# A chunked RWKV scan: the odd chunks' results in the other head's half of the partitions, and the small couplings in two parts

## Chip, core and metric

The kernel runs on one core of a Trainium2 chip. The metric is the device time of one execution in microseconds. TensorE is called PE here and VectorE DVE; ACT is ScalarE, POOL is GpSimd, and SP issues the loads.

## What is computed

The kernel runs a small model end to end: a transformer layer with pooling and neighbourhood attention, a layer with an RWKV mixer, and two conformer layers, over 512 latent and 256 context tokens of width 1024. The change touches the RWKV scan alone. For each of 16 heads (64 wide) and for both time directions the reference does this, first over the context, then over the latent tokens, which alone give an output:

```
def wkv_scan(s0, decay, k, v, kk, a, r, reverse):
    ...
    def step(S, inp):
        w_t, k_t, v_t, kk_t, kka_t = inp[:5]
        S = (S * w_t[:, :, None, :]
             - jnp.einsum('bhij,bhj->bhi', S, kk_t)[..., None] * kka_t[:, :, None, :]
             + v_t[..., None] * k_t[:, :, None, :])
        y = jnp.einsum('bhij,bhj->bhi', S, inp[5]) if emit else None
        return S, y
    S, ys = lax.scan(step, s0, xs, reverse=reverse)
```

## The kernel before

The 768 tokens are cut into 12 chunks of 64 (`C`). The heads are taken in 8 pairs; the two heads of a pair (`h`) lie in the two halves of the 128 partitions, `half(h)`. A pair has three groups (`g`) of four chunks: group 0 is the context, groups 1 and 2 are latent. `t` counts the 24 groups of all pairs. The chunks of a group are in two tiles `q` of two; `pos` is the parity of a chunk within its tile. The two directions `d` walk through the chunks in opposite order, so at each step of the scan they stand at chunks of opposite parity.

Two kinds of work are interleaved, in an order that `rwkv_steps` writes out by hand. For each of 12 places `k` it issues `prep(t, 0, k)`, then one part of `scan(t - 1, ...)`, then `prep(t, 1, k)`, then features of the next head pair and the readout of the last. Every engine goes through the same order, in its own queue, and waits on semaphores.

`prep` makes what a group needs without knowing the state. At k = 0 PE computes the small couplings (L1763: 8 matmuls of 64x64, each with its rows and its output in `half(h)`), which DVE copies through a mask into `xt` (L3569), and then the big ones (L1773: 8 matmuls from 64 rows into all 128 columns), which DVE multiplies by a mask into `couple` (L3579, in the context group L3581), one instruction for each head. At k = 1 PE transposes the small ones (L1814), which ACT copies (L2472), and multiplies the masked couplings with the values (L1787), which ACT copies to `bv` (L2449). From k = 2 to 9 a triangular inverse is doubled level by level: PE product (L1823), DVE masked copy (L3587), PE products (L1836, L1840), ACT copy (L2459). Its last level works on quarters of a block (L1827, L1851), with copies by ACT (L2466) and DVE (L3595). `home(level, h, pos)` says in which half of the partitions the inverse of a chunk lies after a level. For odd chunks it alternates from level to level; at `FULL_STEPS` = 4 it is `h`.

`scan` takes one step of four in three parts. Part 0: PE multiplies the state with the keys, the from-state product (L1864, 4 matmuls into bank 6), and DVE adds `bv` to make the residual `w_sb` (L3613). Part 1: PE multiplies it with the inverse (L1874), and ACT copies the result into `uv` (L2480). Part 2: PE computes the update of the state (L1886) and, in latent groups, the output `y` in bank 7 (L1893, L1898); DVE adds to the state (L3620, L3622) and takes y from its bank (L3628 or L3632), which signals `y_read`. The step's place k for part 0 is 0, 3, 6 or 9.

The features use L1907, L1914 and L1920 on PE, L3646, L3693 and others on DVE. A matmul of f32 shows in the trace as two weight loads and two matmul records, so 4 matmuls are x8.

## Time and profile before

| | us |
|---|---|
| median of 3 runs | 4571.34 (4560.85 to 4578.11) |
| the profiled execution | 4574.23 |
| its span, first to last instruction | 4572.4 |
| PE busy, weight loads busy | 4407.4, 3153.2 |
| DVE busy, ACT busy, POOL busy | 2697.3, 1026.2, 253.7 |
| mean granted clock of TensorE | 0.987 |

Busy times are sums over the span. The ends of matmuls are modelled, so the weight loads (PEld) show better when PE was issuing. The scan is one stage of the span, from 1340 to 1977 us.

### The profile page before, as it was taken

Reading aid. Unit: us, or ns where it says so; the run is one execution under the profiler, and the core shown is the slowest. Engines: PE = TensorE matmul, PEld = TensorE weight load, DVE = VectorE, ACT = ScalarE, POOL = GpSimd, SP = SyncE. Lnnn points to the kernel's source line nnn. Section 1 sums busy time; section 2 is a strip of 40 time slices with the busy share of each in tenths; the row PEclk is TensorE's granted clock in tenths of the full one; section 3 lists DMA queues with packets and bytes.
Section 4 is the critical chain, followed back from the end, with each engine's and each line's share of the span. In section 5 each row is a group of like instructions: output and inputs, shape, how many; then the busy total and the mean of one; then the engine's idle time right before and its main releaser. Section 6 shows DMA issues by size and latency. Waiting matters only on the chain.

```text
span 4572.4 us, 76195 instructions
## 1 busy us (share of the span) xinstructions
PE 4407.4 (96%) x32648; PEld 3153.2 (69%) x32648; DVE 2697.3 (59%) x4804; ACT 1026.2 (22%) x2222; POOL 253.7 (6%) x355
## 2 busy tenths in 40 slices
PE   8999999999999999999999999989999999989998
PEld 4555655555547777768886888557886888556887
DVE  3173555536348888745565666655667666664656
ACT  1063000002037666630002100341001100251000
POOL 0001000001001111110000000210000000120000
PEclk9999999999999999999999999999999999999999
DMA  5320222211200000122221222212222222212221
GB/s 213 132 81 37 92 111 111 110 56 56 88 1 4 4 4 4 40 84 74 93 92 70 82 92 83 74 56 74 93 88 88 77 90 83 92 38 85 81 92 46
DMA packets 27071, 339.47 MB, mean 74 GB/s; under 512 B 3024, under 2 KB 3024, under 8 KB 6896
## 3 DMA queue, kind: packets, MB, share of 16 engines
q1 hardware_dynamic: 24048, 324.51, 18.8%
q0 software_dynamic: 2688, 10.09, 0.6%
q8 instruction: 259, 4.24, 0.4%
q14 instruction: 76, 0.62, 0.0%
HBM read 330.40 MB, written 4.19 MB: 73 GB/s over the span
## 4 chain that ended last, share of the span: by engine, by line
PE 87%; DVE 7%; ACT 3%; issue 2%; DMA 0%; SPq 0%; DVEq 0%; ACTq 0%
PE ps L1624 48%; PE ps L1233 21%; PE ps L1242 2%; PE ps L1286 1%; PE ps L1773 1%; PE ps L1387 1%; ACT arena L2216 1%; PE ps L1480 1%; PE ps L1557 1%; PE ps L1703 1%; PE ps L1907 1%; PE ps L1836 1%; PE ps L1448 1%; PE ps L1513 1%; PE ps L1460 1%
## 5 line engine op out<-in xcount | busy, mean ns | idle before, releaser
L1624 PE MATMUL ps<-arena 128*128 128x256 f32 (+1 forms) x9096 | 2102.4, 393 | 1.8 <-DVE arena L3243 1.8
L1624 PEld LDWEIGHTS ps<-arena 128*128 128x128 f32 x9096 | 1725.8, 190 | 365.4 <-issue 12.4
L1233 PE MATMUL ps<-arena 128*128 128x512 f32 (+3 forms) x2816 | 997.9, 515 | 0.4 <-DVE arena L2819 0.4
L1233 PEld LDWEIGHTS ps<-arena 128*128 128x128 f32 x2816 | 524.3, 190 | 460.0 <-issue 396.6
L3234 DVE TENSOR_TENSOR arena<-ps,arena 128x512 f32<-128x512 f32 (+1 forms) x250 | 157.5, 630 | 302.7 <-PE ps L1624 300.8
L3234 DVE TENSOR_TENSOR square<-ps,square 128x512 f32<-128x512 f32 (+1 forms) x145 | 99.1, 683 | 174.4 <-PE ps L1624 174.4
L3175 DVE TENSOR_TENSOR arena<-arena 128x1024 f32<-128x1024 f32 (+2 forms) x153 | 190.5, 1245 | 3.3
L2383 ACT COPY square<-ps 128x512 f32<-128x512 f32 (+1 forms) x65 | 37.2, 572 | 648.6 <-PE ps L1624 581.4
L2383 ACT COPY arena<-ps 128x384 f32<-128x384 f32 (+1 forms) x35 | 18.6, 530 | 577.5 <-PE ps L1624 546.5
L2459 ACT COPY arena<-ps 128x512 f32<-128x512 f32 x192 | 110.7, 586 | 68.2 <-PE ps L1840 64.8
L3243 DVE TENSOR_TENSOR arena<-arena 128x1024 f32<-128x1024 f32 (+1 forms) x60 | 72.5, 1208 | 86.9 <-ACT square L2383 76.7
L1624 PE MATMUL ps<-arena,square 128*128 128x256 f32 (+1 forms) x432 | 122.0, 431 | 0.0
L2216 ACT ACTIVATE arena<-arena,state_sum 128x256 f32<-128x256 f32 (+3 forms) x128 | 76.5, 601 | 195.3 <-DVE state_sum L2800 195.2
L1242 PE MATMUL ps<-arena 128*128 128x256 f32 (+1 forms) x336 | 105.2, 475 | 15.1 <-DVE arena L3018 8.4
L1167 POOL COPY square<-const 128x256 f32<-128x256 f32 x144 | 80.4, 560 | 700.9 <-PE ps L1840 472.0
L3234 DVE TENSOR_TENSOR reset<-ps,square 128x512 f32<-128x512 f32 (+1 forms) x65 | 43.9, 675 | 127.5 <-PE ps L1624 127.5
L2374 ACT ACTIVATE reset<-arena 128x256 f32<-128x256 f32 x40 | 16.7, 417 | 420.2 <-DVE arena L3308 420.2
L3230 DVE TENSOR_TENSOR arena<-arena 128x1024 f32<-128x1024 f32 (+2 forms) x100 | 107.6, 1076 | 3.4
L3249 DVE TENSOR_TENSOR arena<-arena 128x1024 f32<-128x1024 f32 (+2 forms) x100 | 107.0, 1070 | 1.1
L1624 PEld LDWEIGHTS ps<-arena,square 128*128 128x128 f32 x432 | 82.1, 190 | 33.3
L2746 DVE SCALAR_TENSOR_TENSOR arena<-arena,vec 128x512 f32<-128x512 f32 x120 | 103.5, 901 | 1.3
L1086 POOL TENSOR_TENSOR arena<-arena 128x512 f32<-128x512 f32 x60 | 72.0, 1200 | 566.4 <-ACT arena L2183 559.8
(395 smaller groups left out, 5123.2 us busy)
## 6 DMA issues: line engine op xcount, KB each, us to landing
arena<-in_panels SPq DMA_DIRECT2D x144, 2048.0 KB, 7.7
arena<-in_panels SPq DMA_DIRECT2D x9, 1536.0 KB, 6.4
arena<-in_bias POOLq DMA_DIRECT2D x8, 512.0 KB, 4.3
arena<-in_x_in SPq DMA_DIRECT2D x1, 3072.0 KB, 10.7
x_save<-arena POOLq DMA_DIRECT2D x1, 2048.0 KB, 7.5
arena<-x_save POOLq DMA_DIRECT2D x1, 2048.0 KB, 14.0
out_x<-arena SPq DMA_DIRECT2D x8, 256.0 KB, 2.9
arena<-in_panels SPq DMA_DIRECT2D x1, 1792.0 KB, 11.6
```

The costliest lines, as they stand in the source:

```text
L1167: pool.tensor_copy(step_sb[d][level % 2], unit).then_inc(sem("step_unit"), one("step_unit"))
L1233: ins = pe.matmul(dest, left(k), right(k), start=(k == 0), stop=(k == nk - 1))
L1242: ins = pe.matmul(bank[:, 0:b - a], w[:, k, m * P:(m + 1) * P], src[:, k, a:b], start=(k == 0), stop=(k == KD - 1))
L1624: ins = pe.matmul(bank[:, j * cut.side:(j + 1) * cut.side], left[:, k, j * P:(j + 1) * P], right[k], start=(k == 0), stop=(k == cut.rows - 1))
L2216: act.activation(p_h, p_h, ACT.Exp, bias=soft_at(i, h, NEGMAX), scale=-1.0, accum_out=soft_at(i, h, SUM)).then_inc(sem(f"exped{h}"), one(f ...
L2459: act.copy(both_sb[par][d], both_banks(d)[:, :, P:3 * P].rearrange("p a (w x) -> p a w x", w=2)).then_inc(sem(f"x_ready{d}"), one(f"x_read ...
L2746: ins = dve.scalar_tensor_tensor(conv_y[:, c, :], src, w, conv_y[:, c, :], ALU.mult, ALU.add)
L3175: ins = dve.tensor_tensor(part, x[:, rows], y[:, rows], op)
L3230: dve.tensor_tensor(a21, left_block(w, 0, 0, c), a21, ALU.subtract).then_inc(sem("left"), one("left"))
L3234: dve.tensor_tensor(out, product_of(tile(), cut), other, ALU.add).then_inc(sem("tile_free"), one("tile_free"))
L3243: dve.tensor_tensor(a11, left_block(total, 0, 0, cut), a11, ALU.subtract).then_inc(sem("tile_free"), one("tile_free"))
L3249: dve.tensor_tensor(a12, a12, a11, ALU.subtract).then_inc(sem("left"), one("left"))
```

## The change

The results of odd chunks (`pos` = 1) move to the other half of the partitions: `home` is shifted by one level, so that it is `h ^ 1` at `FULL_STEPS` (`crossed`). The values, the last level of the inverse, the residual and the solve follow. The from-state product of direction d goes to bank 6 + d, so its four matmuls have four different pairs of input and output half; DVE reads the residual from two banks. Bank 7 is the one that holds y, and PE now waits for `y_read` before it writes there. The small couplings of even chunks stay ahead of the big ones; those of odd chunks, whose output lies in the other half, come behind them, after a wait for the first part. `small{d}` counts twice in each group, and DVE's masked copy waits for both.

```diff
@@ -712 @@
+        def crossed(h, pos):
+            return home(FULL_STEPS, h, pos)
@@ -732 @@
         def home(level, h, pos):
-            return h if pos == 0 else h ^ level % 2
+            return h if pos == 0 else h ^ (level + 1) % 2
...
         def plain_at(level, h, pos):
-            return h if level == 0 else home(level - 1, h, pos)
+            return home(max(level - 1, 0), h, pos)
@@ -1757 @@
                     bank = misc("small", t, d)
-                    for q, e, pos, c in places(d, g):
-                        o = (2 * q + pos) * C
-                        for h in range(2):
-                            ins = pe.matmul(ps[half(h), bank, o:o + C], bk[d][half(h), c // 2, 2 * e + pos, :],
-                                            kk_part(p % 2, d, c, h), start=True, stop=True)
-                    ins.then_inc(sem(f"small{d}"), one(f"small{d}"))
+                    def small(of):
+                        for q, e, pos, c in places(d, g):
+                            o = (2 * q + pos) * C
+                            for h in range(2):
+                                if pos == of:
+                                    ins = pe.matmul(ps[half(home(0, h, pos)), bank, o:o + C], bk[d][half(h), c // 2, 2 * e + pos, :],
+                                                    kk_part(p % 2, d, c, h), start=True, stop=True)
+                        ins.then_inc(sem(f"small{d}"), one(f"small{d}"))
+
+                    small(0)
 
                     if t > 0:
                         pe.wait_ge(sem(f"z_ready{d}"), 2 * t)
...
                     ins.then_inc(sem(f"big{d}"), one(f"big{d}"))
+
+                    pe.wait_ge(sem(f"small{d}"), 2 * t + 1)
+                    small(1)
@@ -1784 @@
-                            ins = pe.matmul(ps[half(h), 2 * d + pos, q * C:(q + 1) * C], couple[d][rows, 0, h, 2 * q + pos, :],
+                            ins = pe.matmul(ps[half(crossed(h, pos)), 2 * d + pos, q * C:(q + 1) * C], couple[d][rows, 0, h, 2 * q + pos, :],
                                             uv[par][d][rows, q, e, half(h)], start=True, stop=True)
@@ -1824 @@
-                        ins = pe.matmul(ps[shifted(C * h, second), 2 * d + pos, q * C // 2:(q + 1) * C // 2],
+                        ins = pe.matmul(ps[shifted(C * crossed(h, pos), second), 2 * d + pos, q * C // 2:(q + 1) * C // 2],
                                         left[rows, second], right[rows, first], start=True, stop=True)
@@ -1847 @@
-                    rows = shifted(C * h, second)
-                    ins = pe.matmul(ps[shifted(C * h, first), 2 * d, 2 * P + i * C // 2:2 * P + (i + 1) * C // 2],
+                    rows = shifted(C * crossed(h, pos), second)
+                    ins = pe.matmul(ps[shifted(C * crossed(h, pos), first), 2 * d, 2 * P + i * C // 2:2 * P + (i + 1) * C // 2],
                                     lx_sb[d][rows, pos, q, :], xt[t % 2][d][rows, at, q, second], start=True, stop=True)
@@ -1858 @@
                 if part == 0:
                     pe.wait_ge(sem("state"), step + 1)
+                    if n["y"] > 0:
+                        pe.wait_ge(sem("y_read"), n["y"])
                     for d in range(2):
                         q, e, pos, c = place(d, g, s)
                         for h in range(2):
-                            ins = pe.matmul(ps[half(h), 6, d * C:(d + 1) * C], kk_part(p % 2, d, c, h), state[half(h), buf, d, :],
-                                            start=True, stop=True)
+                            ins = pe.matmul(ps[half(crossed(h, pos)), 6 + d, 3 * P:3 * P + C], kk_part(p % 2, d, c, h),
+                                            state[half(h), buf, d, :], start=True, stop=True)
...
-                                            w_sb[half(h), d, :], start=True, stop=True)
+                                            w_sb[half(crossed(h, pos)), d, :], start=True, stop=True)
@@ -3565 @@
-                    dve.wait_ge(sem(f"small{d}"), t + 1)
+                    dve.wait_ge(sem(f"small{d}"), 2 * (t + 1))
@@ -3610 @@
-                    dve.tensor_tensor(w_sb[:, :, :], chunked(ps[:, 6, 0:P]), each, ALU.add).then_inc(
+                    dve.tensor_tensor(w_sb[:, :, :], ps[:, 6:8, 3 * P:3 * P + C], each, ALU.add).then_inc(
                         sem("residual"), one("residual"))
```

## Rows read from the trace of the kernel before

**Rows 1.** Windows: core, stretch, its us, busy of PE, PEld, DVE, ACT, POOL (records), clock.
```profile
1340.00:1977.00 637.00, 583.70 (x16838) 446.38 (x16838) 490.54 (x1130) 412.62 (x933) 106.91 (x191) 0.97 0.03 10
```

**Rows 2.** Waits in the scan stage: who waited for whom, us, times, longest.
```profile
PEld ps L1787 <- DVE arena L3579: 6.2, 16, 0.4
```

**Rows 3.** Timeline of one latent group's start: start us, us, engine, line, what, [idle before].
```profile
1597.09 0.55 PEld L1763 LDWEIGHTS ps<-arena 64*64 64x64 f32 x16
...
1597.70 0.97 PEld L1773 LDWEIGHTS ps<-arena 64*128 64x128 f32 x16
...
1597.92 0.45 DVE L3569 COPY_PREDICATED arena<-const,ps 128x256 f32<-128x256 int32 x1
...
1598.79 0.31 PEld L1864 LDWEIGHTS ps<-state,arena 64*64 64x64 f32 x8
1598.79 0.45 PE L1864 MATMUL ps<-state,arena 64*64 64x64 f32 x8
1598.91 1.29 DVE L3579 TENSOR_TENSOR arena<-ps,const 128x512 f32<-128x512 f32 x2 [0.53 <-PE ps L1773]
1599.02 0.55 PEld L1763 LDWEIGHTS ps<-arena 64*64 64x64 f32 x16
...
1600.11 0.28 DVE L3613 TENSOR_TENSOR w<-ps,arena 128x128 f32<-128x128 f32 x1
...
1600.72 0.20 PEld L1814 LDWEIGHTS ps<-const,arena 128*128 128x128 f32 x2
...
1600.85 1.29 DVE L3579 TENSOR_TENSOR arena<-ps,const 128x512 f32<-128x512 f32 x2
1601.09 0.32 PEld L1787 LDWEIGHTS ps<-arena 64*64 64x64 f32 x16 [0.17 <-issue]
...
1601.32 0.21 PEld L1874 LDWEIGHTS ps<-w,arena 64*64 64x64 f32 x8
...
1602.19 0.33 PEld L1787 LDWEIGHTS ps<-arena 64*64 64x64 f32 x16 [0.38 <-DVE arena L3579]
```

**Rows 4.** Chain that ended last, 1545.5 to 1624: start us, us, what.
```profile
1592.01 0.17 PE ps L1864 x6
...
1606.67 0.15 PE ps L1864 x5
```

**Rows 5.** Lines of the scan stage: shapes, count, busy us, mean ns, idle before and releasers.
```profile
L3587 DVE COPY_PREDICATED square<-const,ps 128x256 f32<-128x256 int32 x144 | 63.6, 442 | 40.9 <-PE ps L1823 37.9 <-POOL square L1167 1.5
...
L1864 PEld LDWEIGHTS ps<-state,arena 64*64 64x64 f32 x768 | 31.1, 135 | 7.2 <-issue 2.5 <-DVE state L3606 1.7 <-DVE state L3622 0.3
...
L3569 DVE COPY_PREDICATED arena<-const,ps 128x256 f32<-128x256 int32 x48 | 21.2, 442 | 1.8 <-PE ps L1763 1.1
...
L1874 PEld LDWEIGHTS ps<-w,arena 64*64 64x64 f32 x768 | 20.4, 133 | 17.0 <-DVE w L3613 15.1 <-issue 0.8
```

**Rows 6.** Timeline of a context group's start (the columns of rows 3).
```profile
1571.81 0.54 PEld L1763 LDWEIGHTS ps<-arena 64*64 64x64 f32 x16
...
1575.46 0.76 DVE L3581 TENSOR_TENSOR arena<-ps,const 128x256 f32<-128x256 f32 x2 [0.52 <-PE ps L1773]
...
1576.59 0.32 PEld L1787 LDWEIGHTS ps<-arena 64*64 64x64 f32 x16 [0.17 <-issue]
...
1577.07 0.37 ACT L2472 COPY arena<-ps 128x256 f32<-128x256 f32 x1
```

**Rows 7.** Timeline around a from-state product that follows a copy of y.
```profile
1563.91 0.28 DVE L3628 COPY arena<-ps 128x128 f32<-128x128 f32 x1
1564.05 0.31 PEld L1864 LDWEIGHTS ps<-state,arena 64*64 64x64 f32 x8
...
1566.86 0.21 PEld L1874 LDWEIGHTS ps<-w,arena 64*64 64x64 f32 x8 [1.43 <-DVE w L3613]
```

**Rows 8.** The same chain as in rows 4, at a group's start in which DVE comes late.
```profile
1547.24 0.36 DVE arena L3569
...
1550.67 0.46 PE ps L1787 x16
```

## Prediction, made before the changed kernel was run

> **What bounds the kernel now.** I read the views in this order: the windows, to find how much of the span the change can touch; the waits inside that stage; the timeline of one chunk group; the chain that ended last. All matmuls that change lie in the scan stage, 1340 to 1977 us, 637 of 4572.4 us [rows 1]. There PE is busy 583.70 us by the modelled ends, but its weight loads only 446.38, and DVE is busy 490.54. So PE is not simply full: it runs in short bursts and hands over to DVE and ACT between them. The waits say to whom: its loads stood still for 6.2 us, in 16 places, for DVE's coupling mask L3579 [rows 2]; the rows by line add 15.1 us for the residual L3613, and for the state only 1.7 us [rows 5]. The stage is 24 chunk groups (8 head pairs, 3 groups each), each some 25 us long, and in each the three engines take turns. A nanosecond taken from PE counts only where the chain of work that ended last runs through PE at that place.
>
> **What one burst costs.** I count each matmul as two records, since an f32 product is loaded twice: 4 matmuls are x8. The from-state product (L1864, x8) uses two of the four 64x64 quarters of the array and takes 0.23 us from its first load to the next line's (1598.79 to 1599.02). The coupling values (L1787, x16, all four quarters) take the same 0.23 us for twice the records (1601.09 to 1601.32) [rows 3]. So four quarters halve the time: x8 costs 0.11 instead of 0.23. The small couplings (L1763, x16, two quarters) take 0.61 us to the first load of the big ones. Eight of the 16 are 0.23, so the other eight and the change of tile shape are 0.38, of which some 0.15 is the change of shape.
>
> **Part 1, the product from the state: the gain.** The two directions always stand at chunks of opposite parity, so with the odd chunk crossed over, the four matmuls of a step fall into four quarters and two banks. There are 96 steps. The most this can give is 96 x (0.23 - 0.11) = 10.6 us, rounding 0.11 kept. But it counts only on the chain. In a whole head pair (1546 to 1624, 12 steps) the chain names L1864 at four steps, of which two rows stand here [rows 4]. At two of the four it is the step inside the k = 0 burst (as at 1598.79 [rows 3]), which part 2 covers. At 1592.01 and 1606.67 PE work follows it, and the saving reaches ACT's copy. At the other eight the chain is on DVE or ACT: the masked copy of the first direction, a reciprocal, an activation. So I keep 2 x 8 x 0.11 = 1.8 us.
>
> The residual L3613 now reads two banks instead of one. The trace has no such residual, but the masked copy L3587 reads two banks and L3569 one, both 128x256, at 442 ns each [rows 5]. I take zero for it; had it a price, it would be DVE time in 96 places, and 10 ns each would be 1 us.
>
> The inverse, the values, the last half product and the solve only exchange halves: the number of matmuls, their shapes and the quarters in use stay the same, and both layouts already occur today, at levels 0 and 1. Zero, with nothing that must hide it.
>
> **Part 2, the small couplings in two parts: the cost.** Today DVE's copy L3569 starts when the small couplings are there, and runs beside the big ones: it lies at +0.83 us from the start of the burst (1597.92 after 1597.09), the mask L3579 can start only at +1.82 when the big ones are done, and DVE stands idle 0.53 us between [rows 3]. So this copy is free now. After the change the second half of the small couplings comes behind the big ones, and the copy waits for it. I lay out one group, with zero at its first small load. PE: first half 0 to 0.38, big to 1.47 (1.09, as 1597.70 to 1598.79), second half to 1.70, from-state product to 1.81. Then direction 1: first half to 2.19, big to 3.28, second half and change of shape to 3.66, where today it is 3.63. So PE itself is even. DVE: eight such records are finished 0.45 us after their first load and DVE starts 0.05 later, so the first copy starts at 1.47 + 0.50 = 1.97. The mask follows 0.36 later (the share of L3569 in a chain that is all DVE [rows 8]), at 2.33, the residual 1.20 later, 3.53, and then the second copy at 3.28 + 0.50 = 3.78 (DVE would be ready at 3.73). The second mask runs 4.14 to 5.44 (1.30), and the values matmul of direction 1 (L1787) starts at 5.48. Today it starts at 1602.19, which is 5.10. Behind this wait stand, on PE's queue, all of the next level's matmuls, and on DVE the features: all move by 0.38. The wait of PE for this mask exists in 16 places [rows 2], the two latent groups of each of 8 pairs: 16 x 0.38 = 6.1 us.
>
> In the context group the masks are half as long (0.76 for two). There the values of direction 1 start at +4.78 (1576.59 after 1571.81), and PE isn't waiting for DVE. By the same layout the mask ends at 4.90, and those values move by 0.17, to 4.95. But ACT, which must copy their result, is busy with L2480 and L2472 until 1577.44, and the chain goes through ACT [rows 6]. Zero there, but 0.03 of PE: 8 x 0.03 = 0.2 us.
>
> The new wait of PE between big and second half is for its own first half, finished 0.45 us after its start while the big ones load for 0.97: satisfied long before, so nothing. Its price without that cover would be the 0.45 us.
>
> **Part 3, the wait for y_read.** The from-state product now also writes the bank from which DVE takes y. DVE's copy of y follows the state in its queue. At most steps DVE is done with y before PE comes. At one step in each pair PE starts while y is still being copied (L3628 from 1563.91 for 0.28, L1864 at 1564.05): there it starts 0.19 us later, with 0.05 for the hand-over. Queued behind it on PE are the two level-3 products of direction 1 and the halves L1827. But PE then idles 1.43 us for the residual, which DVE reaches only after its features [rows 7]. Zero; uncovered it would be 8 x 0.2 = 1.6 us.
>
> **Sum.** +6.1 + 0.2 - 1.8 = +4.5 us. The profiled execution took 4574.23 us (span 4572.4 and 1.83 around it), so 4578.7 on its own terms. That execution lay 2.9 us above the median 4571.34 of the three shown, which gives 4575.8, so 4576 us.
>
> The Trainium skill, "TensorEngine Tiling (Array Packing)", section Key Properties, says that changing the tiling mode drains the engine. The trace agrees: 0.15 us at small to big. The change adds one such switch in each of 24 groups, from the second half to the transposes. The page alone would count them all, 24 x 0.15 = 3.6 us; in the layout above they lie inside DVE's lag.
>
> **The rivals.**
> A: the whole gain is kept and the copy is hidden. For it: DVE idles 0.53 and 0.52 us before masks [rows 3, 6]. Against it: that idle lies in front of the very point to which the copy moves, so it is used up by the copy's new wait. It gives 4571.3 - 10.6 = 4561 us.
> B, the slower side: DVE's lag at k = 0 is not 0.38 once but both copies in full, in all 24 groups, and the change of shape too. That would be 24 x (2 x 0.44 + 0.15) = 24.7 us, 4596 us. It decides if the big products are ready before DVE comes to them at both directions, context groups included. For it: in every third group DVE comes late to the burst (L3728, then L3569 at 1547.24) and the chain is all DVE from there to the values [rows 8]. Against it: DVE waits 0.52 us for PE in the context group [rows 6].
> C: the four quarters don't run side by side, or what they give is nowhere on the chain, and only the cost stays: 4571.3 + 6.3 = 4577.6, say 4578 us. For it: L1874, x8 over four quarters, has 20.4 us of loads against 31.1 of L1864 [rows 5], so they should; the chain is the weak link. The Trainium skill, same page, section PSUM Bottleneck, says that tiling speeds up TensorE but not the emptying of PSUM. By it the saving would vanish everywhere, with this same result; the trace agrees at eight of twelve steps.
>
> **How the numbers follow.** Forecast 0.60, its own range 4566 to 4586 (the two kept steps could be six or none, the lag 0.2 to 0.5 us in 16 to 24 groups, and the three runs before lie between 4560.85 and 4578.11). A 0.15, B 0.10, C 0.15, where C lies within the forecast's range. The range to 8 in 10 is 4561 to 4590: it takes in A's end and leaves B out. A measurement of this kernel can tell 0.5%, 22.9 us, from no change: below 4548.5 would be faster, above 4594.2 slower. A does not reach the first; B's end lies just beyond the second. So faster 0.03, same 0.90, slower 0.07.
>
> **What would show it.** After the change: L1864's loads, x8, some 0.20 us in a burst instead of 0.31; L3569 at about +1.97 from the first L1763, without idle DVE time between it and the first mask; the wait of L1787 for L3579 grown from 0.38 to about 0.75 at 16 places; the stage about 4 us longer than 637. Wrong if the wait at L1787 doesn't grow (the copy is hidden: A), if it grows in the context groups too (B), if L1864 stays at 0.31 (C), or if a new wait shows in front of the second half of L1763 or of L1864 with y as its releaser.

## The result, and the profile after

| | before | after |
|---|---|---|
| median of 20 runs, us | 4570.56 (4560.85 to 4578.74) | 4579.84 (4569.53 to 4592.37) |
| profiled execution, its span | 4574.23, 4572.4 | 4576.36, 4574.5 |
| mean granted clock of that execution | 0.987 | 0.988 |
| PE, weight loads, DVE busy in the span | 4407.4, 3153.2, 2697.3 | 4396.6, 3140.8, 2694.2 |

The ratio after to before is 1.0022, with a 95% interval of 1.0016 to 1.0028: +9.3 us by the medians, where +4.5 was forecast. That is below the 0.5% named in the prediction, but clearly not zero. The change makes the kernel a little slower, although PE's loads are shorter by 12 us in the whole span (3153.2 to 3140.8).

The windows of the scan stage show where those went. This row is that of [rows 1], for the kernel after (core, stretch, its us, busy of PE, PEld, DVE, ACT, POOL with records, clock):

```profile
1340.00:1977.00 637.00, 571.55 (x16793) 434.15 (x16794) 486.07 (x1126) 414.18 (x933) 104.84 (x191) 0.97 0.03 10
```

Weight loads fall from 446.38 to 434.15 us, in a stage that is not shorter. The rows by line name the places. The line numbers have moved: L1769 is the small couplings (before L1763), L1877 the from-state product (L1864), L1887 the solve (L1874), L1798 the values (L1787), L3582 the masked copy (L3569), L3592 the coupling mask (L3579), L3626 the residual (L3613). Columns: shapes, count, busy us and mean ns, idle before and releasers, as in [rows 5].

```profile
L3626 DVE TENSOR_TENSOR w<-ps,arena 128x128 f32<-128x128 f32 x96 | 27.3, 284 | 7.2 <-PE ps L1877 6.1
L1877 PEld LDWEIGHTS ps<-state,arena 64*64 64x64 f32 x768 | 22.2, 135 | 6.9 <-issue 3.5 <-DVE state L3619 2.1 <-DVE state L3635 0.6
L3582 DVE COPY_PREDICATED arena<-const,ps 128x256 f32<-128x256 int32 x48 | 21.5, 447 | 34.4 <-PE ps L1769 34.4
L1887 PEld LDWEIGHTS ps<-w,arena 64*64 64x64 f32 x768 | 20.8, 135 | 17.5 <-DVE w L3626 15.7 <-issue 0.8
```

The loads of the from-state product fall from 31.1 to 22.2 us, to about those of the solve, which always used four quarters. Ahead of the masked copy DVE stood idle 1.8 us in all 48 places together [rows 5], now 34.4 us. In front of the mask it stood idle 11.3 us before and not at all now, so part of this is the same idle time at another place. The waits of the stage (us in total, times, longest) show what came of it on PE, to be held against [rows 2]:

```profile
PEld ps L1798 <- DVE arena L3592: 12.1, 16, 0.8
...
PEld ps L1798 <- DVE arena L3594: 1.8, 7, 0.3
```

The wait has kept its 16 places and grown from 6.2 to 12.1 us, by 5.9. The timeline of one latent group's start shows the mechanism (start us, us, engine, line, what, idle before):

```profile
1600.62 0.31 PEld L1769 LDWEIGHTS ps<-arena 64*64 64x64 f32 x8
...
1601.00 0.97 PEld L1781 LDWEIGHTS ps<-arena 64*128 64x128 f32 x16
...
1602.09 0.31 PEld L1769 LDWEIGHTS ps<-arena 64*64 64x64 f32 x8
...
1602.66 0.45 DVE L3582 COPY_PREDICATED arena<-const,ps 128x256 f32<-128x256 int32 x1 [1.23 <-PE ps L1769]
1602.76 0.97 PEld L1781 LDWEIGHTS ps<-arena 64*128 64x128 f32 x16
...
1603.00 1.28 DVE L3592 TENSOR_TENSOR arena<-ps,const 128x512 f32<-128x512 f32 x2
1603.85 0.31 PEld L1769 LDWEIGHTS ps<-arena 64*64 64x64 f32 x8
...
1604.42 0.45 DVE L3582 COPY_PREDICATED arena<-const,ps 128x256 f32<-128x256 int32 x1
...
1604.76 1.28 DVE L3592 TENSOR_TENSOR arena<-ps,const 128x512 f32<-128x512 f32 x2
...
1606.09 0.32 PEld L1798 LDWEIGHTS ps<-arena 64*64 64x64 f32 x16 [0.78 <-DVE arena L3592]
```

With zero at 1600.62: first copy at 2.04 (forecast 1.97), first mask 2.38 (2.33), second copy 3.80 (3.78), values of direction 1 at 5.47 (5.48, and 5.10 before). The copy that used to run beside the big couplings now starts when they are over, and the mask comes behind it.

**The account by groups.** These are the first loads of the three groups of one pair and of the next pair, first for before, then for after:

```profile
1495.63 0.55 PEld L1763 LDWEIGHTS ps<-arena 64*64 64x64 f32 x16
...
1520.85 0.54 PEld L1763 LDWEIGHTS ps<-arena 64*64 64x64 f32 x16
...
1545.57 0.55 PEld L1763 LDWEIGHTS ps<-arena 64*64 64x64 f32 x16 [0.76 <-issue]
```

The next pair starts at 1571.81 [rows 6]. After:

```profile
1498.28 0.31 PEld L1769 LDWEIGHTS ps<-arena 64*64 64x64 f32 x8
...
1523.59 0.31 PEld L1769 LDWEIGHTS ps<-arena 64*64 64x64 f32 x8
...
1548.57 0.31 PEld L1769 LDWEIGHTS ps<-arena 64*64 64x64 f32 x8 [0.76 <-issue]
...
1575.42 0.31 PEld L1769 LDWEIGHTS ps<-arena 64*64 64x64 f32 x8
```

Context group 25.22 before, 25.31 after (25.20 in other pairs); first latent group 24.72 and 24.98; second latent group 26.24 and 26.85. So the pair grew from 76.18 to 77.14, by 0.96 us, times 8 is 7.7 us. Other pairs scatter about this: the second latent group has 26.04 to 26.25 us before and 26.68 to 27.12 after. The first latent group grew by 0.26: the lag of 0.38, less the 0.11 of one from-state product on the chain, as forecast. The second grew by 0.61, and that was not forecast. A step of DVE there shows why. It is the sum over the keys, a product of two tiles in SBUF, L3682 before and L3695 after; by line and form, first before, then after:

```profile
L3682 DVE TENSOR_TENSOR arena<-arena 128x512 f32<-128x512 f32 x7 | 4.8, 681 | 0.0
```

```profile
L3695 DVE TENSOR_TENSOR arena<-arena 128x512 f32<-128x512 f32 x7 | 6.3, 903 | 0.0
```

The same work takes 903 ns instead of 681. The timeline shows what runs beside it; the last row of each fence has the shortest, median and longest time of POOL's two copies in ns. Before:

```profile
1554.49 1.65 POOL L1167 COPY square<-const 128x256 f32<-128x256 f32 x2 [12.21 <-PE ps L1840]
...
1555.20 0.68 DVE L3682 TENSOR_TENSOR arena<-arena 128x512 f32<-128x512 f32 x1
...
L1167 POOL COPY square<-const x2: 721/833/945, 1554.5 to 1555.2; 128x256 f32<-128x256 f32 x2
```

After:

```profile
1557.87 1.08 POOL L1170 COPY square<-const 128x256 f32<-128x256 f32 x2 [12.58 <-PE ps L1851]
...
1558.58 0.90 DVE L3695 TENSOR_TENSOR arena<-arena 128x512 f32<-128x512 f32 x1
...
L1170 POOL COPY square<-const x2: 397/566/734, 1557.9 to 1558.5; 128x256 f32<-128x256 f32 x2
```

POOL fills the tile for the next level with the unit matrix as soon as PE's last product of a level is done, for direction 0 first, then for direction 1. Before, the second copy ends at 1556.14 and takes 0.945 us, so it starts at 1555.195, 0.005 to 0.01 us ahead of the sum, and it is the copy that is stretched. After, it ends at 1558.95 and takes 0.397, so it starts at 1558.55, 0.03 ahead of the sum, and it is the sum that is stretched. The two lie beside each other in both kernels; what changed is by how much the copy comes first. PE's last product stands behind the from-state product on PE's queue, so with the shorter one it comes earlier (the records of L1851 end 0.23 us ahead of the sum, those of L1840 before 0.11), while DVE's queue has not moved. Of these 0.12 us the second copy moves by only 0.03; POOL's first copy runs until 0.02 us behind the sum's start in both kernels, which may be what holds it (not shown). In all seven pairs of after the copy is 0.03 us ahead and the sum takes 0.90 us; in before it is 0.01 ahead in six pairs and 0.24 behind in one, and the sum takes 0.68 in all. The run e1, which has the split but not the shorter product, shows the same as before, so it is the crossing that moves the copy. The run e11 tests what the order does.

### The profile page after: what moved, and what is told of

Same layout as the page of the kernel before. It is cut to its first block, busy times and chain, and to the rows that moved or that the text cites. A ratio compares the mean times of both kernels' runs of the same rounds, so it can differ in the third digit from the quotient of the medians.

```text
span 4574.5 us, 76286 instructions
## 1 busy us (share of the span) xinstructions
PE 4396.6 (96%) x32648; PEld 3140.8 (69%) x32648; DVE 2694.2 (59%) x4804; ACT 1027.8 (22%) x2222; POOL 252.1 (6%) x355
## 4 chain that ended last, share of the span: by engine, by line
PE 87%; DVE 7%; ACT 4%; issue 2%; DMA 0%; SPq 0%; DVEq 0%; ACTq 0%
PE ps L1627 48%; PE ps L1236 21%; PE ps L1245 2%; PE ps L1289 1%; PE ps L1390 1%; PE ps L1781 1%; DVE arena L3592 1%; PE ps L1560 1%; PE ps L1483 1%; ACT arena L2229 1%; ACT arena L2472 1%; PE ps L1706 1%; PE ps L1920 1%; PE ps L1451 1%; PE ps L1847 1%
```

## The experiments

Ratios are to the kernel before, run beside each; its medians were 4571.24 (with e0 to e3), 4570.36 (e4 to e7), 4569.95 (e8 to e10) and 4571.31 (e11). The fourth column is the time from the first load of the first of the 24 groups to that of the last, in the profiled execution (before 595.8, after 600.0). The last column is explained below the table.

| run | median us | ratio, 95% | 23 groups, us | over before at equal clock, us (estimate) |
|---|---|---|---|---|
| e0 the change, again | 4582.15 | 1.0020 (1.0010 to 1.0030) | 608.2 | +10.8 (2.0) |
| e1 split alone | 4583.49 | 1.0020 (1.0010 to 1.0030) | 607.3 | +10.8 (1.4) |
| e2 wait for y alone | 4569.78 | 0.9995 (0.9984 to 1.0005) | 593.7 | +1.8 (1.3) |
| e3 all small ones first | 4591.92 | 1.0036 (1.0023 to 1.0049) | 612.1 | +15.3 (2.5) |
| e4 the change, no POOL copies | 4573.48 | 1.0006 (0.9997 to 1.0014) | 593.5 | +3.0 (2.0) |
| e5 before, no POOL copies | 4557.15 | 0.9974 (0.9964 to 0.9984) | 582.3 | -7.0 (1.5) |
| e6 the change, masks first | 4571.98 | 1.0005 (0.9994 to 1.0015) | 594.9 | -1.3 (2.2) |
| e7 the change, key sum moved | 4586.51 | 1.0037 (1.0024 to 1.0049) | 610.8 | +11.5 (1.3) |
| e8 before, masks first | 4576.50 | 1.0018 (1.0009 to 1.0027) | 599.9 | +6.1 (1.4) |
| e9 split alone, masks first | 4571.81 | 1.0012 (1.0002 to 1.0022) | 606.7 | +1.8 (1.9) |
| e10 as e6, again | 4573.49 | 1.0006 (0.9997 to 1.0015) | 598.1 | -0.1 (1.7) |
| e11 the change, a copy later | 4579.21 | 1.0024 (1.0014 to 1.0033) | 607.9 | +7.0 (2.2) |

The fourth column wanders by several us for the same kernel (after 600.0 and 608.2, e6 and e10 594.9 and 598.1). The granted clock is at the lower of its two levels, 1.2 GHz, for short stretches, and a group with such a stretch is longer: in before, a first latent group with 1.7 us of it takes 25.54 instead of 24.72 us, a second latent group with 5.1 us of it 28.22 instead of 26.24. Each execution has them in other places; in the scan stage they add up to 44 us before, 41 after, 58 in e0, 55 in e6 and in e10. So lengths of groups are compared below only where no such stretch falls into them. These are the medians of such groups, in us, without the groups at the two ends of the scan, which differ from the others (a dash where there is none):

| kernel | context | first latent | second latent |
|---|---|---|---|
| before | 25.22 | 24.72 | 26.24 |
| after | 25.20 | 24.98 | 26.85 |
| e1 split alone | 25.37 | 25.27 | 26.80 |
| e2 wait for y alone | 25.22 | 24.72 | 26.26 |
| e5 before, no POOL copies | 25.32 | 24.71 | 25.55 |
| e6 the change, masks first | 25.19 | 24.37 | 26.10 |
| e8 before, masks first | 25.22 | 24.89 | 26.70 |
| e9 split alone, masks first | 25.37 | 24.66 | - |

The clock moves the medians too. In the 102 executions of before that were run beside these, those with a lower mean granted clock took longer, 2.8 us for each 0.001. The last column of the first table is an estimate from this: the mean of a run's executions over that of before beside it, both brought to the same mean clock, with two standard errors in brackets. It takes the clock as given and can't say whether a kernel itself had a part in it.

**e0_changed_again.** The change once more, beside the experiments.

> The changed kernel itself on the same chip, as a yardstick for the others. +7 to +12 us against before by the comparison of 20 runs; by the traces of one execution of each, +4 to +6 us in the scan stage.

4582.15 us against 4571.24: the loss stands, +10.9 by the medians and +10.8 at equal clock.

**e1_split_only.** The split of the small couplings with its two waits, and nothing crossed.

```diff
+                    def small(of):
+                        for q, e, pos, c in places(d, g):
...
+                                if pos == of:
+                                    ins = pe.matmul(ps[half(h), bank, o:o + C], ...
+                    small(0)
...
+                    pe.wait_ge(sem(f"small{d}"), 2 * t + 1)
+                    small(1)
...
-                    dve.wait_ge(sem(f"small{d}"), t + 1)
+                    dve.wait_ge(sem(f"small{d}"), 2 * (t + 1))
```

> The kernel before, with only the small couplings cut in two: even chunks ahead of the big ones, a wait, odd chunks behind them; nothing is crossed over and the from-state product stays in two quarters. Theory 1 (the masked copy loses its cover at k = 0): the second direction's values matmul waits 0.38 us longer for the mask in 16 groups, no gain comes from the from-state product, and no mask or feature of DVE is otherwise moved against POOL: +6 us against before. Rival (the loss comes from the waits for y or from the exchange of halves): +0 to +1 us. Rival B of the prediction (both copies uncovered in all groups): +20 us or more.

4583.49 us, +12.3 (+10.8 at equal clock, as e0): the split alone is as slow as the change. Its waits are those of the change (L1795 is the values there, L3587 the mask):

```profile
PEld ps L1795 <- DVE arena L3587: 12.1, 16, 0.8
```

The start of a latent group shows why more (zero at 1606.40):

```profile
1606.40 0.31 PEld L1766 LDWEIGHTS ps<-arena 64*64 64x64 f32 x8
...
1612.05 0.32 PEld L1795 LDWEIGHTS ps<-arena 64*64 64x64 f32 x16 [0.78 <-DVE arena L3587]
```

The values of direction 1 come at 5.65, not at 5.47: the from-state product between the two bursts still takes 0.23 us, so the second burst, and the copy behind it, come 0.11 later, and the rest goes to small shifts that I didn't separate. The lag is 0.55 us, and the first latent group grows by just that, 25.27 against 24.72. The pair from 1503.38 to 1580.83 lasts 77.45, 1.27 more than before, or 10 us for 8 pairs. So the expectation had the place right and the size too small: of the saving on the from-state product, the part inside the burst does count once the split is there. Held against e1, the change is shorter by 0.17 us in the context group and 0.29 in the first latent one; in the second the stretched sum takes the gain back.

**e2_y_wait_only.** Before, with the wait for the reading of y alone.

```diff
                     pe.wait_ge(sem("state"), step + 1)
+                    if n["y"] > 0:
+                        pe.wait_ge(sem("y_read"), n["y"])
```

> The kernel before, with only the wait for y_read ahead of the from-state product. Theory 1: nothing, within 1 us, since in the one step of each pair where PE comes before y is read it later idles 1.4 us for the residual. Rival: the wait passes through to the end, 8 x 0.2 = 1.6 us or, if PE stands at every latent step, up to 64 x 0.2 = 13 us.

Ratio 0.9995, and groups as long as before (25.22, 24.72 and 26.26). By the groups the wait costs nothing, as forecast. The estimate at equal clock, +1.8 (1.3), would allow the 1.6 us of the rival, but no group shows it.

**e3_both_parts_first.** The change, but both parts of both directions stand ahead of the big couplings, and DVE does both masked copies ahead of the masks. Within a group this should give back what the split costs.

```diff
+                    if d == 0:
...
+                        banks = [misc("small", t, to) for to in range(2)]
+                        for of in range(2):
+                            for to in range(2):
+                                if of:
+                                    pe.wait_ge(sem(f"small{to}"), 2 * t + 1)
+                                small(to, of)
...
+                    for to in range(2) if d == 0 else ():
+                        bank, _ = MISC[("small", t, to)]
...
+                        dve.copy_predicated(flat2(xt[par][to]), unit_mask(to), ...
```

> The changed kernel, with both parts of the small couplings of both directions ahead of the big ones (order: even chunks of direction 0, of direction 1, odd of 0, odd of 1, then big 0, from-state, big 1), and DVE's two masked copies ahead of the masks. Theory 1: the copies lie beside the big products again, the values wait for the mask no longer than before, and the gain of the from-state product stays; 16 x 0.38 and more is won back: 6 to 9 us less than the changed kernel, and 0 to 2 us less than before. Rival (the loss is elsewhere: y, crossing, POOL): as slow as the changed kernel, +9 us against before.

+20.7 us, about 10 worse than the change, where 6 to 9 less were expected: a miss. The waits of PE for the first small load name the cause (times, longest; L3745 is the gate of the last pair's readout, L2518 an activation of ACT):

```profile
PE ps L1765 <- DVE arena L3745: 10.4, 7, 1.7
...
PE ps L1765 <- ACT arena L2518: 3.2, 7, 0.7
```

```profile
1556.24 0.69 DVE L3745 TENSOR_TENSOR arena<-arena,ps 128x512 f32<-128x512 f32 x1
1557.05 1.08 PEld L1765 LDWEIGHTS ps<-arena 64*64 64x64 f32 x32 [2.53 <-issue]
```

The small couplings of direction 1 go to the second of two banks that are given out in turn (`misc`), and its last user is read only by those two steps. When its couplings come behind direction 0's big ones, the bank is free in time; at the head of the burst PE waits. This is a bank's cost and says nothing against the split as such: but the order in which all small ones come first isn't free either.

**e4_changed_no_pool and e5_before_no_pool.** POOL's copies of the unit matrix are left out of the change and of before. The levels of the inverse then work on tiles that are not reset; all other instructions are there.

```diff
-                level, part = divmod(k - 2, 2)
-                if part == 1 and 0 <= level < FULL_STEPS and ...
-                    pool.wait_ge(sem(f"z{d}"), LEVEL_STEPS * t + level + 1)
-                    step_unit(d, level)
...
-                    dve.wait_ge(sem("step_unit"), 2 * (FULL_STEPS * t + level) + d + 1)
+                    dve.wait_ge(sem("step_unit"), min(4, 2 * (FULL_STEPS * t + level) + d + 1))
```

> The changed kernel without the copies with which POOL refills the step tiles during the scan (left out: those copies, so the inverse is computed on stale tiles; times of all other instructions stand). Theory: in the changed kernel one POOL copy falls on DVE's k_sum product in each pair, which takes 0.90 us there instead of 0.68 before; without POOL it is 0.68 again, and this kernel is slower than the same cut of the kernel before by 6 us, not 8 (0.22 x 8 = 1.8 less). Rival: k_sum is longer for another reason and stays at 0.90; the distance stays at 8 us or more.

> The kernel before without the same POOL copies (left out: those copies; times of all other instructions stand). It is the yardstick for the run before it. The copies of before fall on other DVE instructions, so this is 0 to 6 us faster than before; k_sum takes 0.68 us as before.

The key sum in e4 (its L3691):

```profile
L3691 DVE TENSOR_TENSOR arena<-arena 128x512 f32<-128x512 f32 x7 | 4.8, 681 | 0.0
```

It is back at 681 ns, so it is POOL's copy that lengthens it, by 0.22 us. Seven of the 8 pairs have it in the scan (the sum for the first pair lies ahead of it), which is 1.5 us of the loss. The medians can't carry that figure: e4 and e5 lie 16 us apart, more than the change costs with the copies, not less, and e5 is 13 us faster than before where 0 to 6 were expected. Part of it is the clock (0.9876 and 0.9893 in the mean of their runs); at equal clock the distance is 10.0 us, that of e0 and before 10.8, and the errors of both are larger than 1.5. Undisturbed groups are 24.98 and 26.06 to 26.39 us (first and second latent) in e4 and 24.71 and 25.55 in e5, with the context even, so 0.8 to 1.1 a pair, 6 to 9 us. So the stretched sum is shown by its own time in e4, and its share of the kernel's time is an estimate.

**e6_masks_first.** If the cost is that the masked copy stands ahead of the mask on DVE's queue, it should vanish when they change places. Nobody waits at once for the copy but the transpose; so in direction 1 PE also does the values ahead of the transpose, and ACT copies `bv` ahead of it.

```diff
                 if k == 0:
-                    bank, _ = MISC[("small", t, d)]
-                    dve.wait_ge(sem("unit_set"), 2 * t + d + 1)
-                    dve.wait_ge(sem(f"small{d}"), 2 * (t + 1))
-                    dve.copy_predicated(z, unit_mask(d), ...
...
+                    bank, _ = MISC[("small", t, d)]
+                    dve.wait_ge(sem("unit_set"), 2 * t + d + 1)
+                    dve.wait_ge(sem(f"small{d}"), 2 * (t + 1))
+                    dve.copy_predicated(z, unit_mask(d), ...
...
                 elif k == 1:
+                    if d == 0:
+                        turn()
...
+                    if d == 1:
+                        turn()
```

> The changed kernel, with DVE's two masks ahead of its masked copy in both directions, and with the values matmul of direction 1 (and ACT's copy of it) ahead of the transposes. Theory 1: the masks no longer wait behind the copy, so the values of direction 1 start near +4.8 us after the burst's first load instead of +5.48; what then waits is the transposes, to about +5.15, so that the next level starts some 0.2 us earlier in 16 groups: 3 us less than the changed kernel. Rival (DVE's order has no share in the loss): no difference from the changed kernel.

4571.98 us, ratio 1.0005: 8 to 10 us less than the change, where 3 were expected. The timeline (zero at 1602.40; L3595 mask, L3603 masked copy, L1802 values, L1831 transpose):

```profile
1602.40 0.31 PEld L1769 LDWEIGHTS ps<-arena 64*64 64x64 f32 x8
...
1603.99 1.29 DVE L3595 TENSOR_TENSOR arena<-ps,const 128x512 f32<-128x512 f32 x2 [0.79 <-PE ps L1781]
...
1605.19 0.43 DVE L3603 COPY_PREDICATED arena<-const,ps 128x256 f32<-128x256 int32 x1
...
1605.75 1.29 DVE L3595 TENSOR_TENSOR arena<-ps,const 128x512 f32<-128x512 f32 x2
...
1606.96 0.44 DVE L3603 COPY_PREDICATED arena<-const,ps 128x256 f32<-128x256 int32 x1
1607.09 0.32 PEld L1802 LDWEIGHTS ps<-arena 64*64 64x64 f32 x16 [0.27 <-DVE arena L3595]
...
1607.48 0.20 PEld L1831 LDWEIGHTS ps<-const,arena 128*128 128x128 f32 x2
```

The first mask starts at 1.59 instead of 2.38, the values of direction 1 at 4.69 instead of 5.47. The first latent group takes 24.37 us (after 24.98, before 24.72), and the key sum is back at 682 ns: DVE's queue moved too, and the copy now starts 0.07 us behind the sum. This is the strongest evidence for the place of the loss.

**e7_changed_k_sum_moved.** The change, with the key sum and the bonus moved from k = 3 and 6 to k = 7, out of reach of that copy.

```diff
-... 3: [("exp", 1, 0), ("k_sum", 0, 0)],
+... 3: [("exp", 1, 0)],
...
-... 6: [("kr", 1, 2), ("bk", 0, 0), ("bonus", 0, 0)],
+... 6: [("kr", 1, 2), ("bk", 0, 0)], 7: [("k_sum", 0, 0), ("bonus", 0, 0)],
```

> The changed kernel, with the k_sum product and the bonus product after it moved from k = 3 and 6 to k = 7 of the third group of a pair. Theory: POOL's copy no longer meets k_sum, which takes 0.68 us again, and the masked copy behind it starts 0.2 to 0.5 us earlier in 8 groups: 2 to 4 us less than the changed kernel, if k = 7 has room. Rival: the stretch lost to POOL is off the chain, no difference; or k = 7 has no room, up to 8 x 1.4 = 11 us more.

4586.51 us, +16: a miss. The sum takes 878 ns at its new place too, where another copy of POOL has started ahead of it, and the second latent group is 27.20 us long (26.85). That fits the rival, that k = 7 has no room for it on DVE; it was not shown separately.

**e8_before_masks_first, e9_split_masks_first and e10_masks_first_again.** Is e6 faster because of its order alone, and does it need the split and the crossing? e8 is before with the order of e6, e9 is e1 with it, e10 is e6 again.

> The kernel before (one part of small couplings, nothing crossed) with the order of the run e6: DVE's masks ahead of its masked copy, the values of direction 1 ahead of its transposes. Theory: here the copy was free beside the big products, so moving it behind the masks only makes the transposes of direction 1 wait, to about +5.45 us after the burst's first load instead of +4.5: 2 to 6 us more than before. Rival (the order of e6 is better by itself, whatever the split): 5 to 8 us less than before.

> The kernel before with the small couplings in two parts and the order of e6, still with the from-state product in two quarters. Against e6 it lacks only the crossing, so the distance is what the four quarters give. Theory: 0.16 us in the k = 0 burst of 16 groups (the second direction starts 0.12 later, its odd part is late by the same) and 0.11 at one further step in two groups of each pair: 3 to 5 us slower than e6. Rival (the four quarters are nowhere on the chain): equal to e6.

> The run e6 again, beside the two others on the same chip. By the undisturbed groups in the trace of e6 it needs 75.6 us for a head pair where before needs 76.1 and the changed kernel 77.0: 4 us less than before and 11 less than changed; by the medians of e6, 1 to 2 us more than before. Whichever holds, it lies 7 to 11 us under the changed kernel.

In before the new order costs 6.5 us (pair 76.82 instead of 76.18): there the masked copy runs free beside the big couplings, and putting it behind the mask uncovers it. With the split it is the better order: 4571.81 for e9 against 4583.49 for e1. What the crossing then adds, e10 and e6 against e9, lies within the scatter of the medians (+1.7 and +0.2; ratios 1.0006 and 1.0005 against 1.0012). The undisturbed groups do show it: 25.19 against 25.37 in the context and 24.37 against 24.66 in the first latent group, 0.47 us a pair or 3.8 us, of the size that was expected. So the right order of DVE depends on where PE puts the small couplings. By the medians e6 and e10 are level with before, and no version beat it. Their groups would say 0.5 us a pair less than before, 4 us; at equal clock it is 1.3 (2.2) and 0.1 (1.7) us less. Whether the change with masks first is faster than before stays open.

**e11_copy_after_sum.** The change with all of POOL's copies, but the one that meets the sum waits for the residual of DVE, and so comes behind the start of the sum.

```diff
                     pool.wait_ge(sem(f"z{d}"), LEVEL_STEPS * t + level + 1)
+                    if t % GROUPS == 2 and k == 3 and d == 1:
+                        pool.wait_ge(sem("residual"), 4 * (t - 1) + 2)
                     step_unit(d, level)
```

> The changed kernel with one more wait: in the second latent group of each pair, at k = 3, POOL's copy of the unit matrix for direction 1 also waits for DVE's residual of that step. In the changed kernel this copy starts 0.03 us ahead of DVE's sum over the keys, and the sum takes 0.90 us; in the kernel before it starts 0.01 ahead, the sum takes 0.68 and the copy 0.94. The residual ends 0.08 us after the sum's start in DVE's queue, so the copy will now start behind the sum. All of POOL's copies stay. Theory 1, whichever of the two comes first is served first and the other one waits: the sum is back at 0.68 us in all pairs, the copy grows from 0.40 to 0.85 or more, the second latent group is 0.2 us shorter (26.65 instead of 26.85), and the kernel 1.8 us faster than the changed one by the groups, which the medians (4579.8 and 4582.2 before this) may not show. Theory 2, the two slow each other down for as long as they overlap, whoever comes first: the sum stays at 0.85 to 0.90 us, since the copy still lies beside it, and nothing is gained. Theory 3, the sum is lengthened by something else that moved with PE: it stays at 0.90 and the copy at 0.40.

```profile
1565.22 0.68 DVE L3697 TENSOR_TENSOR arena<-arena 128x512 f32<-128x512 f32 x1
1565.43 0.73 POOL L1170 COPY square<-const 128x256 f32<-128x256 f32 x1 [0.19 <-DVE w L3628]
```

The sum is back at 0.68 us, in all seven pairs, although the copy lies beside it for 0.47 us. The copy takes 0.73 instead of 0.40 and ends 0.26 us behind the sum. So theory 1 holds, with the case of before added: a lead of 0.01 us by the records was not enough for the copy, one of 0.035 us was. (The copy grew less than expected, since it starts 0.21 behind the sum; its end is where it was before.) The second latent group takes 26.62 us instead of 26.85 (1555.22 to 1581.84). The median, 4579.21, is level with that of the change, which 1.5 us can't alter visibly; at equal clock it is 3.8 us less than e0, with an error of 3.

## Why the prediction was right, and where its sum was short

**What bounds the stage.** Right. A nanosecond off PE counted only where the chain runs through PE: 8.9 us less of from-state loads, and the stage no shorter.

**Part 2, the lag.** Right in place and size: where the copy's uncovering was laid out, the runs show 16 waits for the mask, +5.9 us where +6.1 stood, each step of the laid-out group within 0.07 us, PE even. e1 shows that the split carries the loss, and e6, e8 and e9 that it is the order on DVE through which it does. Right too that the context group hides it: the seven waits for L3594 there come to 1.8 us, but the group is 25.20 to 25.31 us long, before 25.22. Without the crossing it isn't hidden in full: the context groups of e1 take 25.37.

**Part 1, the gain.** The mechanism is right: in the burst at k = 0 the x8 loads take 0.11 us to the next line's first load, before 0.23. Its sum of 1.8 us was too large. Of the two steps of a pair that I kept, the one in the first latent group counts in full (0.38 - 0.11 = 0.27, measured 0.26). The one in the context group, 1592.01 [rows 4], is not seen in the group's length: six undisturbed groups changed by -0.11 to +0.14, by 0.00 in the mean, where 0.03 - 0.11 = -0.08 was forecast. That is 0.08 us a pair, 0.6 us in all. The chain named the product, but its saving doesn't show at the group's end; into which later wait it went I did not isolate.

**The missed term.** The prediction asked of a shorter PE step only whether the chain moves. It also moved PE against DVE within the group, and with it POOL's copy, from 0.01 us ahead of a DVE instruction, where the copy pays, to 0.03 ahead, where the sum pays: 681 to 903 ns, 0.22 x 7 = 1.5 us. In e4, e6 and e11 the sum is back at 681 to 682 ns. The step that failed is the place of Part 1 where a saving off the chain was worth nothing; POOL's queue waits for the last product of a level, and nothing in the sum followed it.

**Together:** 4.5 + 1.5 + 0.6 is 6.6 us, against 7.7 by the groups of the pair shown and 6.7 by the medians of the undisturbed groups (76.18 and 77.03 a pair). The medians of the kernel say 9.3, with 7.3 to 12.8 by the interval of the ratio. Some of the rest lies in the first pair, whose first latent group is 22.81 us long in before and in e5 and 23.80 in e4, 1.0 more where the others have 0.26. The last 2 us or more stay open; a lower clock is not the reason, since e0 is at +10.8 at equal clock. So the loss is twice the forecast one, and that the time lies in the stated range is owed to the range, 20 us wide, as much as to the sum.

**Part 3 and the residual.** Right: the groups of e2 show nothing for the wait, and the residual takes 284 ns from two banks and 283 before from one.

**The rivals.** A (the copy is hidden) is refuted by the wait of 12.1 us and by e1. B's price of 24.7 us was not reached, since the lag is one copy's start and not both copies in full; its sign, a wait in the context groups, did show (1.8 us in seven places), but without lengthening them. C was half true: the quarters do run side by side, but only one of the two kept steps shows in the length of its group. The rule that I cited beside it, of the Trainium skill, "TensorEngine Tiling (Array Packing)", section PSUM Bottleneck, that tiling speeds up TensorE but not the emptying of PSUM, fits what is seen at this product: its loads fell from 31.1 to 22.2 us, and DVE's residual, which reads the result from PSUM, stayed at 283 to 284 ns. The prediction's "agrees at eight of twelve steps" says only that the chain is on DVE or ACT there, not that emptying PSUM holds it. Nor is the saving lost everywhere: against e1 the crossed form is shorter by 0.17 and 0.29 us in two of three groups.

## What to carry to other kernels

A producer that is cut in two, with the second part behind a longer job, delays its reader by that job; look at what stood in front of the reader's next instruction, and whether the reader's queue should be put in another order with it (masks first: -8 to -12 us with the split, +6.5 without). A saving on an engine off the chain is not neutral: it shifts everything that this engine releases, so follow its releases on every queue, POOL's too, and ask what they start just ahead of. And a bank or a buffer is part of an order: moving work ahead means asking who has still to read the place that it writes (e3).

## What the runs showed of the hardware

DVE's product of two SBUF tiles, 128x512 f32, takes 681 ns alone (e4), and also when a copy of POOL, 128x256 f32 within SBUF, starts 0.21 us behind it (e11), 0.07 behind it (e6) or 0.01 us ahead of it (before). In all three cases the copy ends 0.26 us after the sum, and takes 0.73, 0.87 or 0.945 us. When the copy is 0.03 us ahead (after, e0, e3), it takes 0.397 and the sum 903 ns. So the two did not share a rate; one waited for the other, and a few hundredths of a microsecond decided which. The Trainium skill, "GPSIMD Engine Reference", section Key points, says that POOL shares its SBUF interfaces with VectorE and contends with instructions that have two SBUF inputs. The runs agree, and show for this pair of instructions who pays and how much.

POOL's copies, 106.9 us of an engine that is never the bound, cost before 13 us in all (e5, ratio 0.9974, 0.9964 to 0.9984). By undisturbed groups it is 0.6 us a pair, 5 us, nearly all of it in the second latent group; at equal clock it is 7.0 (1.5) us. The rest goes with the clock, whose mean was 0.9893 in the runs of e5 and 0.9871 in those of before.
